# Expert outputs gathered into the residual by adding transfers, the last expert's rows in two halves and two parts, and the sigmoids moved, in a two-layer decoder kernel

## What is computed

```
for layer in range(2):
    x = x + mixer(rms_norm(x, attn_norm[layer]))
    h = rms_norm(x, ffn_norm[layer])
    # one of 4 groups, in it the 2 best of 4 experts; weights from two softmaxes
    y = 0
    for e in range(16):
        act = silu(h @ w_gate[e]) * (h @ w_up[e])     # 1024 -> 512
        y = y + combine[:, e:e+1] * (act @ w_down[e]) # 512 -> 1024, combine is 0 for 14 of 16
    x = x + y
```

## Time and profile before

| | |
|---|---|
| median of three runs | 1258.27 us (1257.06 to 1258.44) |
| profiled execution: time / span | 1255.91 us / 1253.9 us |
| PE busy | 93% of the span |
| DVE / ACT / POOL busy | 72% / 54% / 16% |
| mean granted TensorE clock | 0.977 |
| bytes moved | 281.75 MB, mean 225 GB/s |

### The profile page before, as it was taken

The page is one execution under the profiler, slowest core; times in us unless marked ns, Lnnn a source line. Parts: engine busy times, 40 slices in busy tenths (PEclk is TensorE's granted clock), DMA queues, the critical chain, the costliest instruction groups (busy, mean ns, idle before and its releaser), DMA issues.

```text
span 1253.9 us, 16896 instructions
## 1 busy us (share of the span) xinstructions
PE 1161.1 (93%) x5788; PEld 885.5 (71%) x5788; DVE 897.8 (72%) x1221; ACT 672.1 (54%) x842; POOL 194.5 (16%) x158
## 2 busy tenths in 40 slices
PE   5999889899799999999968999998979999999996
PEld 4776578778776777777646688887877677777763
DVE  4546568666578888888876247656557988888887
ACT  4335741134357788788743242122425788788772
POOL 1121000010012222222130000001002122212213
PEclk9999999999799999999999999999979999999999
DMA  6231110132599999999950250113168999999976
GB/s 226 93 91 68 67 56 13 68 103 100 204 326 380 380 387 388 383 380 384 384 214 1 71 153 3 67 68 135 67 251 288 379 384 382 391 386 380 384 288 214
DMA packets 129422, 281.75 MB, mean 225 GB/s; under 512 B 18944, under 2 KB 19456, under 8 KB 129360
## 3 DMA queue, kind: packets, MB, share of 16 engines
q1 hardware_dynamic: 119680, 246.98, 54.1%
q0 software_dynamic: 5888, 20.97, 5.3%
q10 hardware_dynamic: 3792, 12.98, 2.6%
HBM read 262.05 MB, written 18.87 MB: 224 GB/s over the span
## 4 chain that ended last, share of the span: by engine, by line
PE 70%; DVE 18%; ACT 4%; issue 4%; DMA 1%; POOL 1%; DVEq 0%; ACTq 0%; POOLq 0%; SPq 0%
PE PS L1146 20%; PE PS L1148 20%; PE PS L1147 19%; DVE expert_w_low L1868 4%; DVE group_low L1653 2%; PE PS L1251 2%; PE PS L1381 2%; PE PS L1409 1%; PE PS L1185 1%; PE PS L1361 1%; DVE AT L1753 1%; DVE hT_low L1637 1%; DVE G L1543 1%; ACT group_high L932 1%; ACT prob L1037 1%
## 5 line engine op out<-in xcount | busy, mean ns | idle before, releaser
L1868 DVE TENSOR_TENSOR expert_w_low<-expert_w,weight_high 128x1024 fp32r<-128x1024 f32 x338 | 407.6, 1257 | 71.9 <-ACT weight_high L908 60.9
L908 ACT ACTIVATE weight_high<-expert_w 128x1024 fp32r<-128x1024 f32 x384 | 375.1, 1048 | 56.0 <-PE PS L1148 48.4
L1146 PE MATMUL PS<-weight_high,xgT_high 128*96 128x512 f32 x512 | 204.5, 399 | 2.6 <-DVEq L1878 2.6
L1148 PE MATMUL PS<-weight_high,xgT_low 128*96 128x512 f32 x512 | 203.3, 397 | 0.0
L1147 PE MATMUL PS<-expert_w_low,xgT_high 128*96 128x512 f32 x512 | 202.3, 395 | 0.0
L1146 PE MATMUL PS<-group_high,hT_high 128*128 128x512 f32 x416 | 170.7, 410 | 13.5 <-DVEq L1640 9.1
L1148 PE MATMUL PS<-group_high,hT_low 128*128 128x512 f32 x416 | 163.8, 394 | 0.0
L1147 PE MATMUL PS<-group_low,hT_high 128*128 128x512 f32 x416 | 163.4, 393 | 0.0
L1653 DVE TENSOR_TENSOR group_low<-group_w,group_high 128x1024 fp32r<-128x1024 f32 x68 | 80.6, 1222 | 50.1 <-ACT group_high L932 47.1
L1146 PE MATMUL PS<-weight_high,actT_high 128*96 128x512 f32 x256 | 102.8, 402 | 8.6 <-DVEq L1926 8.4
L1146 PEld LDWEIGHTS PS<-weight_high,xgT_high 128*96 128x96 f32 x512 | 83.3, 163 | 36.0 <-DVEq L1878 2.7
(11 more groups left out here) (253 smaller groups left out, 1560.7 us busy)
## 6 DMA issues: line engine op xcount, KB each, us to landing
expert_w<-in_moe_w_gate SPq DMA_DIRECT2D x32, 2048.0 KB, 14.1
expert_w<-in_moe_w_up SPq DMA_DIRECT2D x32, 2048.0 KB, 16.2
expert_w<-in_moe_w_down SPq DMA_DIRECT2D x32, 2048.0 KB, 15.0
group_w<-in_even_w_in SPq DMA_DIRECT2D x6, 2048.0 KB, 8.0
group_w<-in_odd_w_in SPq DMA_DIRECT2D x6, 2048.0 KB, 8.5
y_rows<-yb ACTq DMA_DIRECT2D x30, 384.0 KB, 6.1
group_w<-in_even_w_out SPq DMA_DIRECT2D x2, 2048.0 KB, 7.8
h_rows<-h SPq DMA_DIRECT2D x8, 512.0 KB, 10.7
```

Source lines behind the costliest of these rows:

```text
L908: act_(hi, w, ACT.Copy).then_inc(w_hi, 1)
L1146: pe.matmul(out, ah, bh, start=first, stop=False)
L1148: return pe.matmul(out, al, bh, start=False, stop=final)
L1868: tt(lo, w, hi.bitcast(F32), ALU.subtract).then_inc(w_lo, 1)
```

## The change

1. **Adding gathers.** The gathers write into x_sb itself, each as a transfer that adds to what is there (`add_outputs`): first one row for each of the four tiles, then the second row of each, which waits until the tile's first has landed. The buffers yg, the steps "x" and VectorE's 16 additions are gone.
2. **Weights.** Since nothing is left that could multiply by the weight afterwards, ScalarE scales each row when it copies it to yb, by a number per list place (w_slot). To get it, the matmul that makes the lists is twice as wide, and waits for the weights.
3. **Last expert.** Its down product runs over all of the first 512 columns and then over the second, so that the first half is copied while PE does the second. The rows are split into a high part (ScalarE) and a low part (VectorE), and `rows_of_last` is two f32r passes for each half. Tiles 0 and 2 now use banks 4 and 5.
4. **Sigmoids.** "gates" moves from the first unit of q to the third, and all "fk" steps to one place, ahead of "clear".
5. In `head_norm` of the attention, the square reads the copy and no longer PSUM, and the bank is free after the copy. ScalarE's wait ahead of layer 1's second weight group is on the landed rows instead of on the additions.

```diff
-                    fk = ([("gates", l)] if unit[3] == 0 else []) + [("fk", l, unit[3])]
+                    fk = [("gates", l)] if unit[3] == 2 else []
...
-                              14: [("silu", l), ("clear", l)]}.get(n, [])
+                              14: [("silu", l), *(("fk", l, c) for c in range(NH)), ("clear", l)]}.get(n, [])
...
-        return [x[0], x[1], p[0], own[0], stat[0], h[0], p[1], own[1], hT[0], own[2], own[3], stat[1], halves[0], h[1],
-                x[2], p[2], hT[1], stat[2], u[0], h[2], x[3], p[3], hT[2], stat[3], u[1], h[3], hT[3], u[2],
+        return [p[0], own[0], stat[0], h[0], p[1], own[1], hT[0], own[2], own[3], stat[1], halves[0], h[1],
+                p[2], hT[1], stat[2], u[0], h[2], p[3], hT[2], stat[3], u[1], h[3], hT[3], u[2],
...
-                bk.plan(("P", l, i), ([2, 3], [4, 5])[i % 2])
+                bk.plan(("P", l, i), ([4, 5], [2, 3])[i % 2])
...
-            def gather_outputs(l, rows):
-
-                for k in range(2 * NT):
-                    i, c = divmod(k, 2)
-                    if k == 5:
-                        bk.wait_full(pool, ("actT", l), NE - 1)
-                    pool.indirect_dma_start(yg[k][:], None, ybuf[l][0:rows], bass.IndirectOffsetOnAxis(
-                        slot[:, c, i:i + 1], 0)).then_inc(yg_sem[k], 16)
+            def add_outputs(l, rows):
+
+                for c in range(2):
+                    for i in range(NT):
+                        if c:
+                            pool.wait_ge(rows_added[0][i], 16 * (l + 1))
+                        pool.indirect_dma_start(x[:, i], None, ybuf[l][0:rows], bass.IndirectOffsetOnAxis(
+                            slot[:, c, i:i + 1], 0), compute_op=ALU.add).then_inc(rows_added[c][i], 16)
...
                     link(act_(copy.unsqueeze(1), z, ACT.Copy))
-                    link(act_(etmp[:, 0:nbk], z, ACT.Square))
-                    sc.sem_inc(e_ready, 1)
                     sc.sem_inc(bk.freed(key), 1)
+                    act_(etmp[:, 0:nbk], copy.unsqueeze(1), ACT.Square).then_inc(e_ready, 1)
...
-                            sc.wait_ge(x_new, x_count(l - 1, "x", 2))
+                            sc.wait_ge(y_stored, 16 * (NE - 1) * l)
+                            bk.wait_full(sc, ("actT", l - 1), NE - 1)
...
-                        bk.wait_full(sc, key, b)
                         for c in range(2):
-                            link(act_(y_last[0:CAP, c * GC:(c + 1) * GC], PS[0:CAP, 2 + c], ACT.Copy))
-                            sc.sem_inc(y_ready, 1)
-                        sc.sem_inc(bk.freed(key), 1)
+                            if c:
+                                bk.wait_full(sc, key, b)
+                            else:
+                                sc.wait_ge(y_half, l + 1)
+                            act_(y_hi[0:CAP, c * GC:(c + 1) * GC], PS[0:CAP, 2 + c], ACT.Copy).then_inc(y_hi_ready, 1)
...
-                    link(act_(yb[0:CAP].rearrange("p (c n) -> p c n", c=2), PS[0:CAP, 2:4], ACT.Copy))
+                    link(act_(yb[0:CAP].rearrange("p (c n) -> p c n", c=2), PS[0:CAP, 2:4], ACT.Copy,
+                              scale=w_slot[:, bass.ds(b, 1)]))
...
-                for c in range(2):
-                    if i == 0:
-                        pe.wait_ge(y_ready, 2 * l + c + 1)
-                    ins = pe.matmul(PS[:, bk.uses[key][0] + c], lastT[:, i * P:(i + 1) * P],
-                                    y_last[0:CAP, c * GC:(c + 1) * GC], start=True, stop=True)
+                for part, of, ready in ((0, y_hi, y_hi_ready), (1, y_lo, y_lo_ready)):
+                    for c in range(2):
+                        if i == 0:
+                            pe.wait_ge(ready, 2 * l + c + 1)
+                        ins = pe.matmul(PS[:, bk.uses[key][0] + c], lastT[:, i * P:(i + 1) * P],
+                                        of[0:CAP, c * GC:(c + 1) * GC], start=part == 0, stop=part == 1)
...
+                        pe.wait_ge(w_lists, l + 1)
+                    ins = pe.matmul(bank(key)[0:CAP, 0:2 * NE], ohj[:, k], rt["tok"][:, c, i].rearrange("p a n -> p (a n)"),
...
+                    for k, c in [(k, c) for c in range(2) for k in ks] if last else [(k, c) for k in ks for c in range(2)]:
...
+                        if last and (k, c) == (DE // P - 1, 0):
+                            ins.then_inc(y_half, 1)
...
-            def add_gathered(l, i):
-
-                for c in range(2):
-                    k = 2 * i + c
-                    ve.wait_ge(yg_sem[k], 16 * (l + 1))
-                    if c:
-                        ve.wait_ge(x_new, x_count(l, "x", i) - 1)
-                    stt(x[:, i], yg[k][:], rt["wt"][:, c, i:i + 1], x[:, i], ALU.mult, ALU.add).then_inc(x_new, 1)
-
...
-                ve.wait_ge(x_new, x_count(l, "x", i))
+                ve.wait_ge(rows_added[1][i], 16 * (l + 1))
...
+                    if last:
+                        for c in range(2):
+                            ve.wait_ge(y_hi_ready, 2 * l + c + 1)
+                            cols = slice(c * GC, (c + 1) * GC)
+                            link(tt(y_lo[0:CAP, cols], PS[0:CAP, 2 + c], y_hi[0:CAP, cols].bitcast(F32), ALU.subtract))
+                            ve.sem_inc(y_lo_ready, 1)
+                        ve.sem_inc(bk.freed(("down", l)), 1)
...
+                link(tt(r["tok"][:, :, :, 1], r["OH"], r["wt"].unsqueeze(3).broadcast_to(both), ALU.mult))
+                ve.sem_inc(w_lists, 1)
...
+                link(cp(w_slot[:, 0:NE], bank(key)[0:CAP, NE:2 * NE]))
```

More of the change, by code:

```diff
@@ L150, in mixer_steps @@
                     first, second = da[2 * (n - 6)], da[2 * n - 11:2 * n - 10]
-                    ahead, fk = (fk, []) if n == 15 else ([], fk)
-                    steps += stats[:1] + [halves[unit][0]] + ahead + [first] + stats[1:] + fk + [unit] + dT + second
+                    steps += stats[:1] + [halves[unit][0], first] + stats[1:] + fk + [unit] + dT + second
                     steps += {9: [("da norm", l, 0)], 12: [("da norm", l, 1)], 13: [("da norm", l, 2)],
-                              14: [("silu", l), ("clear", l)]}.get(n, [])
+                              14: [("silu", l), *(("fk", l, c) for c in range(NH)), ("clear", l)]}.get(n, [])
             steps += [("cum", l)]
@@ L202, in norm_steps @@
         halves = [("half", *k[1:]) for k in u]
-        x, stat, h, hT = ([(kind, n, i) for i in range(NT)] for kind in ("x", "stat", "h", "hT"))
+        stat, h, hT = ([(kind, n, i) for i in range(NT)] for kind in ("stat", "h", "hT"))
         own = [("split", n // 2, 0, q) for q in range(4)]
@@ L208, in norm_steps @@
         p = [("p", n, i) for i in range(NT)]
[L209 to L210 removed]
+        return [p[0], own[0], stat[0], h[0], p[1], own[1], hT[0], own[2], own[3], stat[1], halves[0], h[1],
+                p[2], hT[1], stat[2], u[0], h[2], p[3], hT[2], stat[3], u[1], h[3], hT[3], u[2],
                 halves[3], u[3]]
[L213 to L214 removed]
     def x_count(l, kind, i):
[L217 to L220 removed]
+        return 2 * NT * l + (NT if kind == "p" else 0) + i + 1
     def with_splits(l, steps):
@@ L356, in build @@
         whi = ar("weight_high", 64, [P, 2, KD, GC], F32R)
-        yg = [at(f"yg{k}", [P, D], F32, o) for k, o in enumerate(
-            [arena + (48 + 4 * k) * KB for k in range(4)] + [ring + 48 * KB, ring + 52 * KB, arena + 68 * KB, arena + 72 * KB])]
-        y_last = ar("y_last", 64, [P, D])
+        zero_rows = ar("zero_rows", 64, [P, D])
+        y_hi, y_lo = ar("y_last_high", 64, [P, D], F32R), ar("y_last_low", 68, [P, D], F32R)
         yb = at("yb", [P, D], F32, ring + 48 * KB)
@@ L435, in build @@
         w_hi, w_lo, w_lo_first = sem("weight_high_ready"), sem("weight_low_ready"), sem("first_low_ready")
-        act_ready, actT_ready, y_ready, y_stored = sem("act_ready"), sem("actT_ready"), sem("y_ready"), sem("y_stored")
-        yg_sem = [sem(f"y_gathered{i}") for i in range(2 * NT)]
+        act_ready, actT_ready, y_stored = sem("act_ready"), sem("actT_ready"), sem("y_stored")
+        y_half, y_hi_ready, y_lo_ready = sem("y_last_first_half"), sem("y_last_high_ready"), sem("y_last_low_ready")
+        w_lists = sem("weights_of_lists_ready")
+        rows_added = [[sem(f"rows_added{c}_{i}") for i in range(NT)] for c in range(2)]
         stored = sem("out_stored")
@@ L1390, in _ @@
                         pe.wait_ge(oh_ready, 2 * l + c + 1)
-                    ins = pe.matmul(bank(key)[0:CAP, 0:NE], ohj[:, k], rt["tok"][:, c, i], start=k == 0, stop=k == 2 * NT - 1)
+                        pe.wait_ge(w_lists, l + 1)
+                    ins = pe.matmul(bank(key)[0:CAP, 0:2 * NE], ohj[:, k], rt["tok"][:, c, i].rearrange("p a n -> p (a n)"),
+                                    start=k == 0, stop=k == 2 * NT - 1)
                 ins.then_inc(bk.filled(key), 1)
@@ L1477, in _ @@
                     pe.wait_ge(bk.freed(("down", l)), bk.uses[("down", l)][1] + NE - 1)
-                    pe.wait_ge(ov_oh[l], 4 * NT)
```

(16 more changed lines are left out.)

74 lines of the change are left out of this document (38 added, 36 removed).

## The result

The changed kernel takes 1265.35 us, median of 5 runs (1263.79 to 1265.93), beside 1257.98 us (1256.58 to 1258.44) for the kernel before. The ratio is 1.0055, 95% interval 1.0043 to 1.0066: slower by 7.4 us. The forecast was 1253.7 and its range ended at 1265.0. The case that came true is the first rival's, for which the prediction had 1262.2 to 1266.9.

The account below looks back on a forecast made before the run. TensorE, busy 93% of the span, was taken as the bound, so only its idle places could pay: 0 - 2.6 - 2.0 = -4.6 us from the profiled 1255.91 gives 1251.3, or 1253.7 us against the median; range 1249 to 1265.

Parts of the forecast that it names:

- first rival: Adding gathers read twice through engines without room, d between 2.2 and 2.72, total 1262.2 to 1266.9 us; chance 0.32.
- d: Time of one adding gather, in both layers; taken as 1.8 us, between bounds of 1.54 and 2.72.
- The upper bound: For an adding gather: both reads one after the other at the weight loads' 385 GB/s, 2.72 us.
- between the layers: Residual additions and norms between layers 0 and 1: 2.6 us saved, with the chain starting 0.65 us later.
- the end: Last gathers, additions and stores of the kernel: last addition ends at 1248.4, span at 1251.9, 2.0 us saved.
- the sum written down for d = 2.72: Both gather places at the slow bound: 2.0 us lost between the layers, 6.6 at the end, +8.6 in all, 1266.9.
- the steps for d = 1.54: Both gather places if the second read is free: 3.7 and 4.3 us saved, -8.0 in all, 1250.3.
- the slope: Each 0.1 us of d costs 1.4 us: five gathers between the layers, eight at the end, more stores ahead.
- The chain behind: Between the layers, from tile 0's first addition to PE's last transposes: shorter by lost VectorE additions and faster last-expert multiplications.
- So the queue costs nothing more: On GpSimd, roots behind waiting second gathers cost nothing, since each is needed only after its own tile's second gather.
- Place 1: Attention ahead of layer 0's recurrence, sigmoids late: taken as 0, between 1.5 us saved and 1.0 lost.
- the fourth rival: In the attention VectorE gets its weight pieces earlier, and Place 1 pays up to 4 us; one in ten.

Follow-up runs that it names:

- e2: The changed kernel with plain gathers that overwrite the residual and don't add to it (result wrong): 1250.11 us, ratio 0.9953 to the kernel before.
- e8: The changed kernel again, unaltered, for a second trace: 1267.84 us, the middle of 2 runs.
- e3: The changed kernel with its gathers reordered in both layers so that tile 0 is whole after three, not five: 1272.09 us, ratio 1.0114.
- e6: e5 with VectorE's four scalings of K and C and the memset moved ahead of its two weight pieces: 1252.57 us, ratio 0.9961.
- e11: The kernel of e6 measured again, beside e10 on one chip: 1250.71 us, ratio 0.9932.
- e5: The kernel before with only the attention's part of the change (late sigmoids, square from the copy), plain gathers kept: 1257.53 us, ratio 0.9993.
- e4: The changed kernel with the last expert's rows whole, in one fp32 tile and one pass, without VectorE's subtraction: 1265.41 us, ratio 1.0057.
- e1: The changed kernel with sigmoids, scalings of K and C and the square put back where they stood before: 1263.63 us, ratio 1.0042.
- e7: The changed kernel with the scalings moved ahead of the weight pieces as in e6: 1257.50 us, ratio 0.9999.
- e9: The changed kernel with e3's gather order between the layers only, tile 0's root ahead of the last gather: 1262.54 us, ratio 1.0043.
- e10: e9 with e7's scalings of K and C ahead of VectorE's weight pieces: 1253.60 us, ratio 0.9965.

## Why the prediction was wrong

**The step that failed is the choice of d.** The prediction says: "I take 1.8: rows, pieces and source are those of the plain gather, so its row is the nearer one", with 0.26 us for the read of the residual. The runs show 2.48 us from landing to landing and 2.79 us by the queue's share, for 1.54 and 1.52 without the addition. The upper bound, both reads one after the other at 385 GB/s (2.72 us), was the nearer row: what the added operand costs isn't hidden behind the plain transfer. The same 1152 packets keep the 16 engines busy for 79.7% of the window in place of 43.5%, and the engines are full while these gathers run (1.06 to 1.07 of the stretch). Against the 0.26 us that I allowed stand 0.94 by landings and 1.27 by shares, although the residual lies on chip. Why the engines need so long, the read itself or the addition with it, stays open. The argument against, that gathers reached 355 GB/s and not 385, spoke of under a tenth of their time.

The Trainium skill's "Collectives: The Full Stack", section "Part 3: Why 7× under link rate — side-by-side accounting", has a reducing transfer of a collective at half a copy's rate for its two reads. The trace agrees with its direction and less with its size: 206 to 211 GB/s where e2's plain gathers got 331 over 646 to 650, which is 0.62 to 0.64, and 0.55 by the queue's shares. Half of the plain gather's own rate would have been d = 3.08. The rule named the effect ahead of the result; the rival that it stood beside had 0.32.

**The rest of the sum, with d as measured.** By the prediction's own steps d = 2.48 gives +0.8 us between the layers and +4.4 at the end; the traces have +3.5 and +4.2. So the end held, and between the layers 2.7 us are missing, see below. That the sum written down for d = 2.72 (+2.0 and +6.6, 8.6 in all) lies near the traces' 7.7 is partly luck: d is smaller, and the missing part makes up for it. (With three stores of 1.30 us ahead of the last landing, as the text has it, that end comes to 7.4 and not 6.6.) By the steps for d = 1.54 it gives -8.0 us; e2's marks have -3.2 between the layers (2.51 to -0.64) and -4.7 at the end (-0.91 to -5.6), 7.9 in all. So the chains of the two places were right, and so is the slope in the main. It was to be 1.4 us for each 0.1 us of d; the 15.2 us between e2 and the changed kernel by medians, for 0.94 us (landings) to 1.27 us (shares) of d, are 1.6 to 1.2.

**Between the layers.** The gather and not the last expert's product starts the chain: right. Tile 0 was to be whole at 639.92 + (d - 1.54) + 4d, which is 650.8 for 2.48, or 652.9 with the 2.1 us that had come in before; it was 655.19. Missing are 2.3 us in this trace and 0.8 in e8's, where tile 0 was whole at 653.59. Two things may make them, and no run tests either: an adding gather takes longer to issue (1.55 to 1.83 us on GpSimd; 0.94 to 1.42 before), and the first gathers ran at 186 to 197 GB/s over 640 to 646. The chain behind, from tile 0's addition to PE's last transposes, was to be 3.25 us shorter than 29.8; it is 2.8 shorter (27.0), and 2.1 in e8. The prediction has no term for PE's clock here. It was 0.50 over 654 to 658, behind PE's wait of 11.78 us, and the first eight transposes took 1.97 us, where the last eight took 1.04.

**"So the queue costs nothing more"** was true of this order, in which roots wait for data anyway. e3 shows how near it was to false.

**The end.** Last addition to the end of the span: 4.4 us after its start at 1259.01, 4.8 before. The plain end isn't a fixed number: from the last weight piece it takes 34.6 us in the profile of before, 35.3 in e6, 36.6 in e11, 37.2 in e5. The changed kernel has 38.8 in both of its traces. So 4.2 us is what two traces say, and 1.6 to 4.2 what these traces together allow.

**Place 1.** The level matmuls were to start at 182.1 behind 5.7 us of idleness, at half the clock; they started at 181.71 behind 5.82, at 0.50. The wait and the clock are as forecast, but the start agrees by luck: this kernel had come in 1.6 us late. In e5, which hadn't, they start at 180.08, 2.8 us earlier than before and not 0.75, since the sigmoids end at 167.6 and not 169.7 and the weight pieces follow; that is the fourth rival's case. The place was taken at 0 and measured at 0 (e5: 0.9993), but not by the sum's terms. On the way it was 2 us ahead: PE's slow stretch (6.12 us in e5 for 3.84) took part of the gain, and the remainder went in later stretches where PE's clock falls in different places. That VectorE's idle 7.57 us stood ahead of the very scalings that PE waited for was in my working ("but what follows waits for VectorE") and I didn't draw the conclusion: e6 is worth 4 to 5 us.

**The rest.** The loop is unchanged: 54 us of PE in 456 to 510, and the marks keep their distance from 413 to 625, so the scaling on ScalarE and the wider product by the list are hidden. Of the 2.1 us ahead of the loop's end, 1.6 come in at a fall of the clock, see the last section; 1.8 go again by 217.78, and 2.3 come in from there to 413, where the clock falls in other places than before (0.73 over 270 to 275 for 1.00). No run shows one of the change's parts as their cause. The halves, for which I counted 1.8 us in the chain, show 0.5 to 1.2 us there beside e4, and nothing in the medians; tile 0's start moves by as much from one execution to the next (1.5 us between the changed kernel and e8).

## What to carry to other kernels

The indirect gather that adds into its destination took 2.48 us here where the plain one took 1.54, and it stood on the path that everything waited for. In return VectorE's additions went, which shortened the chain between the layers by 2 to 3 us. So weigh such a transfer by how long its queue will then hold up the first tile. When a cost isn't in the trace and one bound is a resource that is already full, take that bound. And when an engine idles ahead of work that another engine waits for, look at what stands first in its queue: moving four scalings and a memset ahead of two steps that wait was worth 4 to 5 us.

## What the hardware showed that I had not expected

TensorE's clock fell behind a wait, and in a kernel with the same PE instructions there it didn't. Both kernels hold PE for 1.82 us ahead of 90.6 us; PE's matmuls behind it are the same. The stretches of the kernel before and then of the changed one:

```profile
92.00:93.00 1.00, 1.00 (x6) 0.79 (x5) 0.96 (x3) 0.71 (x4) 0.00 (x0) 1.00 0.00 0
93.00:94.00 1.00, 1.00 (x8) 0.53 (x7) 0.24 (x2) 0.00 (x0) 0.54 (x1) 1.00 0.00 0
```

```profile
92.00:93.00 1.00, 1.00 (x4) 0.81 (x3) 0.96 (x3) 0.78 (x4) 0.00 (x0) 0.50 0.07 16
93.00:94.00 1.00, 1.00 (x4) 0.71 (x4) 0.31 (x2) 0.00 (x0) 0.46 (x1) 0.50 0.00 0
```

The clock is 1.00 in the one and 0.50 in the other, from about 91.3 to 94.6, and the mark at 102.53 comes 1.6 us later. It is the same in the changed kernel, e1, e2, e3, e4, e7, e8 and e9 (1.62 to 1.74 us), and absent in before, e5, e6, e10 and e11 (0.04 to 0.18 us). e10 has adding gathers, halves and late sigmoids all three, so they don't make the fall by being there. What decides it stays open. A sum of stretches is off by such a step even where the instructions are the same. At this place it repeats in the two pairs of traces of one kernel (the changed kernel and e8, e6 and e11), so that a second trace doesn't average it away. It isn't so everywhere: the marks of e6 and e11 part by 1.5 us between 217.78 and 261.72, and those of the changed kernel and e8 by 3.2 us between 674.60 and 852.96.
